# Index scores of a sparse-attention step: sample pairs on column groups, two prompt heads on row halves, shorter accumulator clearing

## The reference

```python
def index_scores(q_i, k_i, w_i):
    s = jnp.einsum('bthd,bsd->bths', q_i, k_i, preferred_element_type=jnp.float32) * (IDX_DIM ** -0.5)
    return jnp.einsum('bths,bth->bts', jax.nn.relu(s), w_i.astype(jnp.float32))
...
# prompt, per block of 128 queries
sc = index_scores(qib, k_i, wib)
sc = jnp.where(kpos[None, None, :] <= qpos[None, :, None], sc, -jnp.inf)
# sample: each sequence scores its own 1024 cached keys, then its own 8 new ones (causal)
sc = jnp.concatenate([index_scores(q_i, past_ik, w_i),
                      jnp.where(causal[None], index_scores(q_i, k_i, w_i), -jnp.inf)], axis=-1)
```

## Time and profile before

| what | us |
|---|---|
| median of three runs | 3414.61 |
| the profiled execution | 3416.94 |
| its span | 3415.40 |
| PE busy in it | 3218.2 (94%) |
| DVE busy in it | 1714.6 (50%) |
| ACT busy in it | 760.4 (22%) |
| score stage, from PE's first score matmul to its last | 229.45 to 289.78 |
| first matmul of the projection loop | 300.02 |

### The profile page before, as it was taken

The page is one execution under the profiler, slowest core; times in us unless marked ns, Lnnn a source line. Parts: engine busy times, 40 slices in busy tenths (PEclk is TensorE's granted clock), DMA queues, the critical chain, the costliest instruction groups (busy, mean ns, idle before and its releaser), DMA issues.

```text
span 3415.4 us, 52518 instructions
## 1 busy us (share of the span) xinstructions
PE 3218.2 (94%) x20665; PEld 3015.6 (88%) x20676; DVE 1714.6 (50%) x2425; ACT 760.4 (22%) x1214; POOL 251.7 (7%) x409
## 2 busy tenths in 40 slices
PE   5878999999999999999999998799978899999997
PEld 4656999999999999999999998667755699999997
DVE  4544778711233345555555554456533453654654
ACT  4221000012000111211111111443422333433332
POOL 3000000000000000000000000122113201010000
PEclk8989999999999999999999999899998999999998
DMA  9723222222221223333232322742157676584672
GB/s 322 254 82 95 64 69 75 69 75 63 68 75 56 88 64 93 92 89 107 75 111 83 107 75 74 246 109 73 30 168 225 205 239 180 169 263 128 202 201 80
DMA packets 522863, 422.02 MB, mean 124 GB/s; under 512 B 19835, under 2 KB 491131, under 8 KB 519491
## 3 DMA queue, kind: packets, MB, share of 16 engines
q1 hardware_dynamic: 500044, 338.53, 34.7%
q0 software_dynamic: 22720, 82.20, 6.5%
HBM read 346.96 MB, written 75.81 MB: 124 GB/s over the span
## 4 chain that ended last, share of the span: by engine, by line
PE 89%; DMA 4%; DVE 3%; ACT 1%; issue 1%; SPq 1%; DVEq 0%; POOL 0%; ACTq 0%; POOLq 0%
PE banks L278 18%; PE banks L280 18%; PE banks L279 18%; PE banks L1486 6%; PE banks L1488 6%; PE banks L1487 6%; PE banks L678 4%; PE banks L711 3%; PE banks L700 1%; DMA ada_w<-in_w_ada 1%; PE banks L333 1%; DMA u_raw<-in_w_out 1%; PE banks L1039 1%; PE banks L2026 1%; PE banks L2022 1%
## 5 line engine op out<-in xcount | busy, mean ns | idle before, releaser
L278 PE MATMUL banks<-h_hi,w_hi 128*128 128x352 f32 (+2 forms) x3744 | 1226.7, 328 | 12.3 <-DVE w_lo L269 10.3
L280 PE MATMUL banks<-h_hi,w_lo 128*128 128x352 f32 (+2 forms) x3744 | 1222.1, 326 | 0.0
L279 PE MATMUL banks<-h_lo,w_hi 128*128 128x352 f32 (+2 forms) x3744 | 1221.1, 326 | 0.0
L278 PEld LDWEIGHTS banks<-h_hi,w_hi 128*128 128x128 f32 (+1 forms) x3744 | 701.5, 187 | 17.2 <-issue 15.9
L279 PEld LDWEIGHTS banks<-h_lo,w_hi 128*128 128x128 f32 (+1 forms) x3744 | 703.8, 188 | 1.3
L280 PEld LDWEIGHTS banks<-h_hi,w_lo 128*128 128x128 f32 (+1 forms) x3744 | 700.7, 187 | 1.3
L269 DVE TENSOR_TENSOR w_lo<-w_raw,w_hi 128x2048 fp32r<-128x2048 f32 (+1 forms) x79 | 180.0, 2279 | 640.7 <-ACT w_hi L265 532.0
L304 ACT ACTIVATE col<-banks 128x384 f32<-128x384 f32 x150 | 71.2, 475 | 1027.5 <-PE banks L280 1027.5
L1536 DVE MAX8 best<-work 128x8 f32<-128x1088 f32 x224 | 289.4, 1292 | 10.8 <-issue 1.0
L1538 DVE MATCH_REPLACE8 work<-best,work 128x1088 f32<-128x1088 f32 x224 | 285.9, 1276 | 0.0
L265 ACT CAST w_hi<-w_raw 128x2048 fp32r<-128x2048 f32 (+1 forms) x79 | 150.0, 1899 | 583.0 <-PE banks L280 538.5
(11 more groups left out here) (240 smaller groups left out, 3320.7 us busy)
## 6 DMA issues: line engine op xcount, KB each, us to landing
w_raw<-in_w_in SPq DMA_DIRECT2D x78, 1024.0 KB, 5.7
u_raw<-in_w_out SPq DMA_DIRECT2D x96, 512.0 KB, 5.3
scratch_proj<-col POOLq DMA_DIRECT2D x78, 544.0 KB, 3.0
ada_w<-in_w_ada SPq DMA_DIRECT2D x16, 2048.0 KB, 13.7
u_raw<-in_w_pb SPq DMA_DIRECT2D x48, 512.0 KB, 4.8
gate_w<-in_w_ada SPq DMA_DIRECT2D x16, 1024.0 KB, 7.6
u_raw<-in_w_pa SPq DMA_DIRECT2D x48, 256.0 KB, 3.0
gates<-scratch_proj SPq DMA_DIRECT2D x64, 192.0 KB, 2.4
```

What stands on the lines that cost most here:

```text
L278: nc.tensor.matmul(dst, w_hi[:, par, k, 0:width], h_hi[:, k, a:b], start=(k == 0), stop=False)
L279: nc.tensor.matmul(dst, w_hi[:, par, k, 0:width], h_lo[:, k, a:b], start=False, stop=False)
L280: mm = nc.tensor.matmul(dst, w_lo[:, par, k, 0:width], h_hi[:, k, a:b], start=False, stop=(k == KT - 1))
```

## The change

For the prompt tiles, two heads are now computed side by side. The keys stand on both halves of the partitions (`ki_two`), and each matmul takes only the 64 partitions of its head, for the queries and for the keys, where before it took 128 with zeros on the idle half. The matmuls of heads h and h+1 alternate in program order, into PSUM banks that come from `pick_bank`: four sets of two banks for the prompt, two sets of three for the sample. A pair waits for the ReLU of the head two before it.

For the sample tile, a pair of sequences now has 16 rows of its own in a group of 32 rows (rows 32j to 32j+15, the other 16 of the group hold zeros or what was left there). Its four matmuls no longer accumulate: each writes 32 rows of PSUM, one group of 32 columns of the array. The new tokens' keys are done the same way with 16 columns each. The tile thus has 128 rows, and `mask_i`, the head weights and the later load of the picks (`keep_sf`) follow that layout, the last with four DMAs for one.

`acc` is filled with -BIG only beyond the width of the tile, without a semaphore; the two clearings of the keys' idle halves are gone; the query block matrix is half as large and takes 8 copies instead of 32.

```diff
-    t["mask_i"] = np.where(ok, 0.0, -BIG).astype(np.float32)
+    t["mask_i"] = np.zeros((P, SMP), np.float32)
+    for r in range(SMP):
+        t["mask_i"][r // 16 * 32 + r % 16] = np.where(ok[r], 0.0, -BIG)
...
-        ki_hi = at("ki_hi", [P, TOK], F32, W0 + 32768)
-        ki_lo = at("ki_lo", [P, TOK], F32, W0 + 37120)
+        ki_two = at("ki_two", [P, TOK], F32, W0 + 32768)
...
-        qi_pair = at("qi_pair", [P, IH, NB // 2, SMP], F32, W0 + 50176)
+        qi_own = at("qi_own", [P, IH, NB // 2, 32], F32, W0 + 50176)
...
+        pick_bank = lambda n: 3 * (n % 2) if PICKS[n // IH] == QT else 2 * (n % 4)
...
-            sp.dma_start(keep_sf[:], scr["keep"][len(PICKS) - 1, 0:SMP, :]).then_inc(smp_landed, 16)
+            for j in range(NB // 2):
+                sp.dma_start(keep_sf[16 * j:16 * j + 16, :], scr["keep"][len(PICKS) - 1, 32 * j:32 * j + 16, :])\
+                    .then_inc(smp_landed, 16)
...
-            nc.vector.memset(ki_hi[ID:P, :], 0.0)
-            nc.vector.memset(ki_lo[0:ID, :], 0.0)
-            nc.vector.memset(qi_pair[:], 0.0).then_inc(idx_zeroed, 1)
+            nc.vector.memset(qi_own[:], 0.0).then_inc(idx_zeroed, 1)
...
-                    for j in range(NB // 2):
-                        c0 = (2 * j + b) * NT
-                        last = nc.vector.tensor_copy(qi_pair[ID * b:ID * b + ID, h, j, c0:c0 + NT], src[:, j, b, :])
+                    last = nc.vector.tensor_copy(qi_own[ID * b:ID * b + ID, h, :, b * NT:(b + 1) * NT], src[:, :, b, :])
...
-                nc.vector.memset(acc[:, j % 2, :], -BIG).then_inc(acc_fill, 1)
-                dve.wait_ge(acc_fill, j + 1)
-                out = acc[0:rows, j % 2, 0:width]
+                if width < TOK:
+                    nc.vector.memset(acc[:, j % 2, width:TOK], -BIG)
+                out = acc[:, j % 2, 0:width]
...
+            for j in range(NB // 2):
+                tr = nc.tensor.matmul(banks[32 * j:32 * j + 16, 5, QT * IH:TT * IH],
+                                      wi_r[:, SEQ + 16 * j:SEQ + 16 * j + 16], ident[0:IH, 0:IH], start=True, stop=True)
...
-            for t in PICKS:
-                rows, width = ROWS_OF(t), WIDTH_OF(t)
-                for h in range(IH):
-                    need(pe, relu_set, n - 1)
-                    keys = (ki_hi, ki_lo)[h % 2]
+            for t in PICKS[:-1]:
+                width = WIDTH_OF(t)
+                for h0 in range(0, IH, 2):
+                    need(pe, relu_set, n - 2)
                     for a in range(0, width, 512):
                         b = min(a + 512, width)
-                        dst = banks[0:rows, 3 * (n % 2) + a // 512, 0:b - a]
-                        if t < QT or a == PAST:
-                            mm = nc.tensor.matmul(dst, qi_t[:, h // 2, t * P:t * P + rows], keys[:, a:b],
+                        for h in (h0, h0 + 1):
+                            half = slice(ID * (h % 2), ID * (h % 2) + ID)
+                            mm = nc.tensor.matmul(banks[:, pick_bank(n + h % 2) + a // 512, 0:b - a],
+                                                  qi_t[half, h // 2, t * P:(t + 1) * P], ki_two[half, a:b],
                                                   start=True, stop=True)
-                        else:
-                            for j in range(NB // 2):
-                                mm = nc.tensor.matmul(dst, qi_pair[:, h, j, :], past_t[:, j, a:b], start=(j == 0),
-                                                      stop=(j == NB // 2 - 1))
-                    mm.then_inc(score_done, 1)
-                    n += 1
+                            if b == width:
+                                mm.then_inc(score_done, 1)
+                    n += 2
+            for h in range(IH):
+                need(pe, relu_set, n - (h > 0))
+                half = slice(ID * (h % 2), ID * (h % 2) + ID)
+                for a in range(0, PAST, 512):
+                    for j in range(NB // 2):
+                        nc.tensor.matmul(banks[32 * j:32 * j + 32, pick_bank(n) + a // 512, :], qi_own[:, h, j, :],
+                                         past_t[:, j, a:a + 512], start=True, stop=True)
+                for j in range(NB // 2):
+                    c0 = SEQ + 16 * j
+                    mm = nc.tensor.matmul(banks[32 * j:32 * j + 16, pick_bank(n) + 2, 0:SMP], qi_t[half, h // 2, c0:c0 + 16],
+                                          ki_two[half, SEQ:TOK], start=True, stop=True)
+                mm.then_inc(score_done, 1)
+                n += 1
```

More of the change, by code:

```diff
@@ L182, in decode_step @@
         diag = at("diag", [P, P], F32, W0 + 67488)
-        mask_i = at("mask_i", [SMP, SMP], F32, W0 + 68000)
+        mask_i = at("mask_i", [P, SMP], F32, W0 + 68000)
         acc = at("acc", [P, 2, TOK], F32, W0)
@@ L1582, in index_scores @@
                     if h == 0:
-                        nc.vector.tensor_scalar(out, relu_s[0:rows, n % 2, 0:width], wi_tok[0:rows, t, h:h + 1], None,
+                        nc.vector.tensor_scalar(out, relu_s[:, n % 2, 0:width], wi_tok[:, t, h:h + 1], None,
                                                 ALU.mult).then_inc(acc_step, 1)
                     else:
-                        nc.vector.scalar_tensor_tensor(out=out, in0=relu_s[0:rows, n % 2, 0:width],
-                                                       scalar=wi_tok[0:rows, t, h:h + 1], in1=out, op0=ALU.mult,
+                        nc.vector.scalar_tensor_tensor(out=out, in0=relu_s[:, n % 2, 0:width],
+                                                       scalar=wi_tok[:, t, h:h + 1], in1=out, op0=ALU.mult,
                                                        op1=ALU.add).then_inc(acc_step, 1)
                     n += 1
-                tail = acc[0:rows, j % 2, width - rows:width]
+                own = mask_i if t == QT else diag
+                tail = acc[:, j % 2, width - ROWS_OF(t):width]
                 dve.wait_ge(acc_step, n)
-                nc.vector.tensor_tensor(tail, tail, mask_i[:] if t == QT else diag[:], ALU.add).then_inc(acc_set, 1)
+                nc.vector.tensor_tensor(tail, tail, own[:], ALU.add).then_inc(acc_set, 1)
         @block.sync
@@ L1637, in _ @@
             sp.dma_start(qi_t[:], scr["proj"][0:2].rearrange("m p n -> p m n")).then_inc(idx_landed, 16)
-            sp.dma_start(ki_hi[0:ID, :], scr["proj"][2, 0:ID, :]).then_inc(idx_landed, 16)
-            sp.dma_start(ki_lo[ID:P, :], scr["proj"][2, 0:ID, :]).then_inc(idx_landed, 16)
+            for x in range(2):
+                sp.dma_start(ki_two[ID * x:ID * x + ID, :], scr["proj"][2, 0:ID, :]).then_inc(idx_landed, 16)
             sp.dma_start(wi_r[:], scr["proj"][2, ID:ID + IH, :]).then_inc(idx_landed, 16)
@@ L1775, in _ @@
                     need(act, acc_step, n - 1)
-                    nc.scalar.activation(relu_s[0:rows, n % 2, 0:width],
-                                         banks[0:rows, 3 * (n % 2):3 * (n % 2) + 3, :].rearrange(
-                                             "p b n -> p (b n)")[:, 0:width],
+                    nc.scalar.activation(relu_s[:, n % 2, 0:width], flat(pick_bank(n), P, width),
                                          ACT.Relu, scale=IH ** -0.5 * ID ** -0.5).then_inc(relu_set, 1)
@@ L2004, in _ @@
             pe.wait_ge(idx_landed, 6 * 16)
[L2005 to L2008, removed]
+            for t in range(QT):
+                nc.tensor.transpose(banks[:, 5, t * IH:(t + 1) * IH], wi_r[:, t * P:(t + 1) * P], ident[0:IH, 0:IH])
+            for j in range(NB // 2):
+                tr = nc.tensor.matmul(banks[32 * j:32 * j + 16, 5, QT * IH:TT * IH],
+                                      wi_r[:, SEQ + 16 * j:SEQ + 16 * j + 16], ident[0:IH, 0:IH], start=True, stop=True)
             tr.then_inc(wi_turned, 1)
```

5 lines of the change are left out of this document (2 added, 3 removed).

## The result

Measured beside the kernel before, the changed kernel took 3391.68 us (median of 4 runs, 3389.87 to 3397.10) against 3413.32: a ratio of 0.9938, 95% interval 0.9921 to 0.9955. Two later measurements of the same kernel on other chips gave 0.9908 (0.9893 to 0.9922) and 0.9921 (0.9907 to 0.9934). It is faster by 21 to 31 us. I had said 3389.7, 24.9 less than before; the time lies in the range.

What follows compares the result with a forecast made beforehand. PE was taken to bound the first and last prompt tiles and the sample, DVE the middle tiles. Savings of 24.5 us through the scores and 0.4 behind gave 24.9, so 3389.7 us, range 3385.5 to 3395.0.

Steps and rivals of the forecast that it cites:

- Part 1: Until the first score matmul: cheaper query copies start it at 227.3 us against 229.45, 2.15 us saved.
- Part 2: Prompt tiles: DVE bounds them, fills cost 3.19 us less, PE's sample work starts at 254.9 us against 261.6.
- Part 3: Sample tile: column groups overlap, 2.05 us a head, 2.0 us lost to the clock; scores end at 265.3 against 289.78.
- Part 4: Behind the scores: loop starts 10.24 us later, its 1.2 GHz stretch saves 0.4 us, extra pick loads cost nothing.
- all later stages of the old length: Expected sign of the forecast: stages behind the scores keep their duration; a move above 2 us would count against it.
- the sum: Whole kernel: 24.5 us saved by the end of scores plus 0.4 behind them, 24.9 us in all.
- 1: Rival, prompt tiles: the row halves don't overlap, 3392.4 to 3394.4 us; chance 12%.
- 4: Rival, sample tile: column groups run one after another, heads of 7.0 us again, 3407.3 us; chance 3%.
- 2: Rival, score stage: PE's clock never falls, 2.0 us less, 3387.7 us; chance 13%.
- 3: Rival, score stage: PE's clock stays at 1.2 GHz through most of it, 3397 us; chance 9%.
- 5: Rival, score stage: the divided array neither overlaps nor keeps the clock, 3465 us; chance 1%.
- 6: Rival, score stage: heads and sample still go one by one, about 3410 us; chance 2%.

Runs made afterwards that it cites:

- full fill: Changed kernel with the old fill of `acc` (1088 columns in every tile) and its semaphore wait: scores 40.7 us, ratio 0.9946 to the kernel before.
- whole rows: Changed kernel, but each prompt matmul takes all 128 rows with zeros on the idle half: scores 39.9 us, ratio 0.9934 to the kernel before.
- sample as before: Changed kernel with the old sample tile (64 rows, accumulating matmuls, 32 copies, one load of picks): scores 56.4 us, ratio 1.0000 to the kernel before.

## Why the prediction was right

The mechanism held: each part of the stage moved as it was said to. That the number came so close is in part luck, since terms were off in both directions. The score stretch is 35.6 us where the prediction had 38.0 (227.3 to 265.3). Of the 24.2 us by which the traced span is shorter, 1.4 come from ahead of the mask's load, 27.6 from the stage and the loop behind it (26.0 and 1.6), and 2.0 from the end of the kernel; the sample attention took 6.8 back.

- **Part 1**, until the first score: 2.15 us said, 1.4 measured from the mask's issue in the first trace and 0.8 in two later ones. A copy of four times the columns costs 0.19 us, where I took 0.13; it lies outside my bounds of 0.10 and 0.17, and makes 0.5 us. The masks landed 0.3 us later after their issue in the first trace (6.6 us against 6.3), and 0.9 and 1.0 later in the other two (7.2 and 7.3), where I had put 0 and at most 0.5. In those two this is the larger miss.
- **Part 2**, prompt tiles: sample work of PE said 27.6 us after the first score, measured 25.6. DVE bounds the tiles and its fills were on the path (full fill, +5.1). The term mis-sized is the fill: I took only its shorter length (3.2 us). In the two timelines a fill and the multiply behind it take 4.3 us less over the five tiles (the first multiply-add starts 0.81 to 0.92 us after the fill does, for 1.59 to 1.89), since without the semaphore the multiply starts under the fill; and of the 0.18 us ahead of each fill, 0.02 on the mean is left, 0.8 us in all. The five later tiles took 22.3 us (231.85 to 254.12) where I had 24.1. The overlap of halves, which no row before showed, is real (whole rows, +5.9 at the sample's start). What I said of the kernel before, that DVE bounds its middle tiles, is half of it: its chain runs over PE from 243.33 us on, and with whole rows the short fills brought only 0.7 us.
- **Part 3**, sample: 10.4 us said, 10.0 measured. The heads at full clock took 8.4, as worked out; the clock cost 1.6 for the 2.0 said, and the idle wait ahead of it was 3.07 for "nearly 4"; with that wait at 0.63 us the clock didn't fall. The earlier trace rows were the right model: four groups of columns in a later stage gave the price of these.
- **Part 4**, behind: the gap was 10.4 us for 10.24, and the loop's stretch at 1.2 GHz about 4.3 us (272.6 to 276.9) for 5.2 said and 6.0 before. The four loads of picks show no cost: from the loop's first matmul to the sample attention it is 2208.3 us for 2209.9.
- What I had wrong was "all later stages of the old length": the sample attention was 6.8 us longer in the first trace, at a lower clock. By my own sign (a later stage moves by more than 2 us) that counts against me. The three measurements of the changed kernel saved 21.6, 31 and 26 us by their medians, around the 24.9 of the sum; the stages behind the scores scatter by enough for that, but which of them made the difference between the medians isn't shown, as each has one trace only.

Of the rivals, 1 is out by whole rows and the row at 247.13, 4 by the sample as before, 2 and 3 by the clock's one fall of about 3.4 us in the sample, and 5 and 6 by the score stretch of 35.6 us. What the Trainium skill gives for three column tiles in "TensorE: Matmul & The Clock Gate", Measured speedup vs the span model (2.38 for 3), isn't what four did here: 16 passes took 1.85 us in the chain, a factor of 3.7 against 6.87, and the whole head 2.1. (My estimate from that figure, 2.2 us for the passes of a head, is 0.5 more than the 1.72 of the sum, so it would have made the sum about 2 us later and not 1.) "TensorEngine Tiling (Array Packing)", Key Properties, says that a change of tiling mode drains the engine. The 0.3 us more a head in the sample as before, where each head changes from 128 rows to 64 and back, agrees with that; no run separates the drain from the smaller matmuls themselves.

## What to carry to other kernels

Matmuls that use half of the rows or a quarter of the columns could here be put side by side, nearly for the price of one, but only enough PSUM banks turned that into time: with two sets instead of four three quarters of the stage's gain were gone (54.4 us against 60.3 and 35.6), part of it by the clock. Where two engines are close to being the bound, one faster engine brings little: look at what DVE does between its real work (fills, semaphores on itself) together with PE's passes, and at waits that cover more banks than they must. When a kernel's time scatters by more than an edit is worth, measure the edit in its stage, and look in more than one trace before you name what scatters.

## What the runs showed of the hardware

- With two bank sets PE stayed at 1.2 GHz for 27 us while it was busy 18.33 of them by its records, in turns with idle stretches of 0.95 to 1.6 us; then it held 2.4 GHz from 252 to about 266 us with idle stretches of 1.6 to 2.0 us. In the changed kernel, busy 13.79 of 17 us, it held 2.4 GHz (a mean of 0.98).
- The sample attention, the same code in 13 traces, took from 174.8 us at a mean clock of 0.88 to 185.3 at 0.81. That alone can move the kernel by 0.3%.
- Eight passes of 512 columns on two row halves took 1.99 us, which is four rounds of 0.43 and the end of the last. A head of 64 columns was about 0.3 us longer (7.26 against 6.99) when its last two passes used 64 rows and not 128.
